# Expert weights in rows of 1024 columns: one change to a two-layer transformer trunk on one core

## The reference

```python
def swiglu(x, w_gate, w_up, w_down):
    return (jax.nn.silu(x @ w_gate) * (x @ w_up)) @ w_down

def moe_swiglu(x, router, w_gate, w_up, w_down):
    logits = (x @ router).astype(jnp.float32)
    top_vals, top_idx = lax.top_k(logits, TOP_K)          # 2 of 8 experts for each frame
    gates = jax.nn.softmax(top_vals, axis=-1)
    combine = jnp.sum(jax.nn.one_hot(top_idx, N_EXPERTS) * gates[..., None], axis=-2)
    y = jnp.zeros_like(x)
    for e in range(N_EXPERTS):
        y = y + combine[..., e:e + 1] * swiglu(x, w_gate[e], w_up[e], w_down[e])
    return y
```

## Time and profile before

| | |
|---|---|
| median of 3 runs | 1616.21 us (1614.83 to 1619.98) |
| the profiled execution | 1619.26 us, its span 1617.5 us |
| TensorE, matmul / weight load | 95% / 80% of the span busy |
| VectorE, ScalarE, GpSimd | 78%, 64%, 8% busy |
| DMA | 484.32 MB, 299 GB/s over the span |
| the expert part, from about 662 us on | 388 GB/s in most slices |

### The profile page before, as it was taken

How to read it: one execution, slowest core, us unless ns; L and a number is a source line. 1 busy time by engine, 2 the same in 40 slices (tenths; PEclk the granted TensorE clock), 3 DMA queues, 4 the chain that set the end, 5 groups by cost and what they waited for, 6 DMA issues and landing times.

```text
span 1617.5 us, 22158 instructions
## 1 busy us (share of the span) xinstructions
PE 1541.0 (95%) x7950; PEld 1286.4 (80%) x7950; DVE 1260.5 (78%) x1224; ACT 1041.4 (64%) x972; POOL 126.6 (8%) x148
## 2 busy tenths in 40 slices
PE   9999999999999898999999999998999998999886
PEld 9888988888896797788888888776887776887664
DVE  5687475555647565789889889899898889898988
ACT  5564444443436443678778777887777887778774
POOL 3103010000104201000000000000000000000220
PEclk9999999999999999899999999999999999999988
DMA  9437856465465462799999999999999999999994
GB/s 356 167 131 239 308 176 221 137 219 187 168 210 181 141 211 66 251 385 335 390 388 387 388 379 369 388 387 387 388 387 388 388 387 387 388 387 389 381 381 173
DMA packets 239042, 484.32 MB, mean 299 GB/s; under 512 B 8352, under 2 KB 11456, under 8 KB 238944
## 3 DMA queue, kind: packets, MB, share of 16 engines
q1 hardware_dynamic: 229744, 454.06, 78.1%
q0 software_dynamic: 7440, 25.83, 4.9%
q10 hardware_dynamic: 1760, 3.15, 0.5%
HBM read 477.21 MB, written 14.18 MB: 304 GB/s over the span
## 4 chain that ended last, share of the span: by engine, by line
PE 61%; DVE 14%; DMA 12%; issue 8%; ACT 3%; POOL 1%; SPq 0%; DVEq 0%; ACTq 0%; POOLq 0%
PE bank L427 16%; PE bank L429 16%; PE bank L428 16%; DVE w_lo L2150 4%; DMA raw<-in_moe_w_up_dram 3%; DMA raw<-in_moe_w_down_dram 3%; DMA raw<-in_moe_w_gate_dram 2%; PE bank L417 2%; PE bank L420 2%; PE bank L419 2%; ACT w_hi L1183 2%; DMA c_add<-gate_rows 2%; DVE w_lo L1593 2%; DVE w_lo_more L2150 1%; PE bank L906 1%
## 5 line engine op out<-in xcount | busy, mean ns | idle before, releaser
L1183 ACT ACTIVATE w_hi<-raw 128x2048 fp32r<-128x2048 f32 (+1 forms) x322 | 608.2, 1894 | 236.5 <-PE bank L429 161.6
L2150 DVE TENSOR_TENSOR w_lo<-raw,w_hi 128x2048 fp32r<-128x2048 f32 x221 | 502.3, 2288 | 69.2 <-ACT w_hi L1183 64.8
L1593 DVE TENSOR_TENSOR w_lo<-raw,w_hi 128x2048 fp32r<-128x2048 f32 (+1 forms) x96 | 211.1, 2203 | 144.4 <-ACT w_hi L1183 144.1
L427 PE MATMUL bank<-w_hi,xe_hi 128*128 128x512 f32 x460 | 182.8, 397 | 0.2
L429 PE MATMUL bank<-w_hi,xe_lo 128*128 128x512 f32 x460 | 179.6, 390 | 0.0
L428 PE MATMUL bank<-w_lo,xe_hi 128*128 128x512 f32 x460 | 179.2, 390 | 0.0
L2150 DVE TENSOR_TENSOR w_lo_more<-raw,w_hi_more 128x2048 fp32r<-128x2048 f32 x63 | 144.1, 2288 | 15.0 <-ACT w_hi_more L1183 9.4
L427 PE MATMUL bank<-w_hi,xT_hi 128*128 128x512 f32 (+1 forms) x384 | 146.9, 383 | 0.1
L429 PE MATMUL bank<-w_hi,xT_lo 128*128 128x512 f32 (+1 forms) x384 | 144.5, 376 | 0.0
L428 PE MATMUL bank<-w_lo,xT_hi 128*128 128x512 f32 (+1 forms) x384 | 144.4, 376 | 0.0
L1183 ACT ACTIVATE w_hi_more<-raw 128x2048 fp32r<-128x2048 f32 x64 | 122.8, 1918 | 23.2 <-PE bank L429 7.9
(11 more groups left out here) (356 smaller groups left out, 3023.1 us busy)
## 6 DMA issues: line engine op xcount, KB each, us to landing
raw<-in_moe_w_gate_dram SPq DMA_DIRECT2D x96, 1024.0 KB, 11.3
raw<-in_moe_w_up_dram SPq DMA_DIRECT2D x96, 1024.0 KB, 11.0
raw<-in_moe_w_down_dram SPq DMA_DIRECT2D x96, 1024.0 KB, 11.4
raw<-in_mem_wkv_dram SPq DMA_DIRECT2D x16, 1024.0 KB, 7.4
raw_more<-in_moe_w_up_dram SPq DMA_DIRECT2D x16, 1024.0 KB, 13.5
raw_more<-in_moe_w_gate_dram SPq DMA_DIRECT2D x16, 1024.0 KB, 10.7
raw_more<-in_moe_w_down_dram SPq DMA_DIRECT2D x16, 1024.0 KB, 12.0
raw<-in_c_w_in_dram SPq DMA_DIRECT2D x12, 1024.0 KB, 5.1
```

The costliest lines, as they stand in the source:

```text
L427: nc.tensor.matmul(d, xh, hi[:, k, :], start=(first and k == 0), stop=False)
L1183: return nc.scalar.activation(dst, src, ACT.Copy)
L1593: tt(w_lo[s][:, 0:n], raw[c % NRAW][:, 0:n], w_hi[s][:, 0:n].bitcast(F32), ALU.subtract).then_inc(lo_made, 1)
L2150: tt(w_lo[s][:, :], raw_exp[r][:, :], w_hi[s][:, :].bitcast(F32), ALU.subtract).then_inc(lo_made, 1)
```

## The change

The expert weights of a chunk become two row tiles by 1024 columns instead of four row tiles by 512. The chunk is as large as before and there are as many; its contiguous rows in HBM are 4 KB. With 1024 columns a chunk feeds two banks: gate blocks 2i and 2i + 1 are filled together by four chunks, then both up blocks by four; in down the left and the right half of the output, banks 4 and 5, fill together over 14 chunks. Seven blocks are three pairs and an odd one, which stays at 512 columns, and so do the down chunks of the last job, whose left half is wanted early.

```diff
+        def gate_up(c):
+            if c < 8 * DBL:                      # DBL = EJ // 2 = 3 pairs, RK = CK // 2 = 2 row tiles
+                up, q = divmod(c % 8, 4)
+                return up, (2 * (c // 8), 2 * (c // 8) + 1), RK * q, RK, q == 0, q == 3
+            up, q = divmod(c - 8 * DBL, 2)
+            return up, (EJ - 1,), CK * q, CK, q == 0, q == 1
...
+                if idx is not None and len(outs) == 2:
+                    both = [w[s][:, :].rearrange("p (k c) -> p k c", k=n) for w in (w_hi, w_lo)]
+                    for k in range(n):
+                        for i, (_, dst) in enumerate(outs):
+                            wh, wl = (w[:, k, i * cols:(i + 1) * cols] for w in both)
...
+                            nc.tensor.matmul(dst[:, :], xh, wh, start=begin, stop=False)
+                            nc.tensor.matmul(dst[:, :], xh, wl, start=False, stop=False)
+                            m = nc.tensor.matmul(dst[:, :], xl, wh, start=False, stop=end)
...
-                    src = w[0][bass.ds(e, 1), k0 * P:(k0 + CK) * P, col:col + W].rearrange(
+                        w, k0, n, col = moe_w_down, RK * (c - 4 * EJ), RK, 0
+                    src = w[0][bass.ds(e, 1), k0 * P:(k0 + n) * P, col:col + CHUNK // n].rearrange(
                         "e (k p) c -> p (e k) c", p=P)
```

More of the change, by code:

```diff
@@ L859, in expert @@
                     idx = N0 + c + EC * job
-                    if c < 2:
-                        pe.wait_ge(emptied[c], start[c] + JOB_CLAIMS[c] * job)
+                    if c == 0:
+                        for b in range(2):
+                            pe.wait_ge(emptied[b], start[b] + JOB_CLAIMS[b] * job)
                     if c == C_INDEX:
@@ L874, in expert @@
                     if c < 4 * EJ:
[L875 to L880, removed]
+                        up, js, k0, _, first_of, last_of = gate_up(c)
+                        outs = [(0, bank[2 * up + j % 2]) for j in js]
+                        if first_of:
+                            for j in js:
+                                claim(pe, f"{z}eu{j}" if up else f"{z}eg{j}", 2 * up + j % 2, job,
+                                      signal=False)
+                        chunk_product(c, outs, xe_hi, xe_lo, k0, first_of, last_of, W, idx=idx,
+                                      slot=E_SLOT[c], done=chunk_used,
                                       packed=(lambda k: xe_two[:, k, :]) if narrow else None)
-                    else:
+                    elif last:
                         i, q = divmod(c - 4 * EJ, EK // CK)
@@ L891, in expert @@
                                       packed=(lambda k: eT_two[:, k, :]) if narrow else None)
-                    if c % 4 == 1 and 1 <= c // 4 <= EJ:
-                        j = c // 4 - 1
+                    else:
+                        q = c - 4 * EJ
+                        if q == 0:
+                            for i in range(2):
+                                claim(pe, f"{z}ed{i}", 4 + i, job, signal=False)
+                        if q % 2 == 0:
+                            wait_emptied(pe, f"{z}et{q // 2}", job)
+                        chunk_product(c, [(0, bank[4]), (0, bank[5])], eT_hi, eT_lo, RK * q, q == 0,
+                                      c == EC - 1, W, idx=idx, slot=E_SLOT[c], done=chunk_used,
+                                      packed=(lambda k: eT_two[:, k, :]) if narrow else None)
+                    if c in C_FOLD:
+                        j = C_FOLD[c]
                         b = 6 + j % 2
@@ L1507, in expert @@
                         nc.scalar.nop().then_inc(emptied[fillings[f"{z}eu{j}"][0]], 1)
-                    if (c == 4 * EJ + EK // CK - 1 or c == EC - 1) and (last or not narrow):
-                        i = (c - 4 * EJ) // (EK // CK)
+                    for i in range(2):
+                        if c != (EC - 1 if i or not last else C_HALF) or (narrow and not last):
+                            continue
                         act.wait_ge(chunk_used, idx + 1)
@@ L2134, in expert @@
                         nc.vector.nop().then_inc(emptied[fillings[f"{z}eu{j}"][0]], 1)
-                    if narrow and not last and (c == 4 * EJ + EK // CK - 1 or c == EC - 1):
-                        i = (c - 4 * EJ) // (EK // CK)
+                    for i in range(2):
+                        if c != EC - 1 or last or not narrow:
+                            continue
                         dve.wait_ge(chunk_used, idx + 1)
```

85 lines of the change are left out of this document (52 added, 33 removed).

## The result

The change made the kernel slower by 0.6%: 1626.98 us (six runs, 1624.55 to 1627.76) against 1618.41 us for the kernel before in the same comparison, a ratio of 1.0058 [1.0047, 1.0069]. Forecast were 1606 and a range of 1595 to 1617. The profiled execution is 1627.3 us long, its span 1625.6.

A forecast was written before the change was run, and what follows sets the result against it. The DMA was taken to pace the pairs n1+w1 and n2+w2, TensorE the wide jobs ahead, VectorE z. Terms -4.4, -6.5, -2, -0.5 and +3.6 gave -9.8, say -10: median 1616.2 becomes 1606, range 1595 to 1617.

The forecast's parts named there:

- The stream: Weight loads in 4 KB rows: 410 GB/s instead of 388; n1 -4.4, n2 -6.5, w1 and w2 together -2 us.
- z: Last job, bound by VectorE with down chunks as before: 0 to -1 us, taken as -0.5.
- Transposed blocks are wanted one for two chunks of down, not one for each: never late: Down chunks: paired chunks want transposed blocks less often, so no wait for them; 0 us.
- The paired evacuations: 0: Bank readouts of paired blocks, followed through steps 19 to 29: 0.7 us or more in hand at each chunk, cost 0.
- VectorE reads both halves at step 41 ... 0: Narrow job's y readout: the same work, 1.4 us passing into the next wide job's start; -1.4 and +1.4, net 0.
- 1.2 us each: ScalarE's second y piece at step 41 of wide jobs delays the starts of n1, n2 and z: 3.6 us in all.
- Slower: Rival, chance 0.07: pairs cost TensorE its lead in wide jobs' three-slot steps, +21 us less the 10: 1627.

The follow-up runs named there:

- rows only: Kernel before, its program kept, most chunks loaded as two row tiles by 1024 columns (weights in wrong places, timing only): 1605.62 us, ratio 0.9922.
- down only: Changed kernel with gate and up back at 512 columns in the old order, only down weights at 1024, both y halves at step 41: 1619.84 us.
- experiment 6: Changed kernel with the odd block folded into bank 3 instead of bank 6, no instruction moved: 1621.21 us, ratio 1.0024 to the kernel before.
- 2 to 7: Changed order with 512-column loads; changed kernel with later odd fold, y behind split, down at 512, bank 3, or bank 3 and y late: 1616.75 to 1631.88 us.
- 1 and 8 to 10: Long rows alone; down alone at 1024; that with y late; the latter with ScalarE's y piece cut to 8 columns: 1605.62, 1619.84, 1612.93, 1613.49 us.
- experiment 7: Kernel of experiment 6, with VectorE reading a narrow job's first y half in step 6 of the following wide job: 1616.75 us, ratio 0.9995.
- experiment 5: Changed kernel with down weights of every job at 512 columns again and y's halves at steps 34 and 41: 1625.03 us, ratio 1.0039.

## Why the prediction was wrong, step by step

**What paces a narrow job.** Its length is VectorE's busy time and VectorE's idle time. In n1 it is busy for 98.7 us with the rows alone and for some 97.6 in the changed kernel, since one half of y has moved out. The idle time of n1 and n2, added up from the gaps between VectorE's instructions in each trace and cut at its splits, shows where each kernel loses:

| us | length | idle | up to the split of chunk 4 | 4 to 19 | 19 to 30 | 30 to 34 | rest |
|---|---|---|---|---|---|---|---|
| n1, rows only | 103.7 | 5.0 | 2.6 | 0.2 | 2.0 | 0.0 | 0.3 |
| n1, down only | 104.2 | 7.1 | 3.9 | 0.9 | 2.0 | 0.0 | 0.3 |
| n1, down at 512 | 109.5 | 10.4 | 2.6 | 0.6 | 4.5 | 2.5 | 0.3 |
| n1, bank 3 | 106.8 | 9.2 | 3.9 | 0.6 | 4.7 | 0.0 | 0.0 |
| n1, changed | 110.9 | 13.3 | 3.9 | 0.6 | 4.7 | 4.1 | 0.0 |
| n2, rows only | 107.4 | 8.7 | 6.2 | 0.2 | 2.0 | 0.0 | 0.3 |
| n2, down only | 108.6 | 11.2 | 7.6 | 0.2 | 2.5 | 0.5 | 0.3 |
| n2, down at 512 | 114.8 | 15.7 | 6.2 | 0.6 | 4.6 | 4.0 | 0.3 |
| n2, bank 3 | 111.1 | 13.4 | 8.2 | 0.6 | 4.7 | 0.0 | 0.0 |
| n2, changed | 114.3 | 16.4 | 8.1 | 1.3 | 4.5 | 2.4 | 0.0 |

**The stream: right.** 403 to 412 GB/s where nothing holds it, n1 103.7 us with the rows alone (103.6 forecast), n2 107.4 (106.5), w1 and w2 119.6 (119). That the median of the rows alone, 1605.6, meets the forecast of 1606 is luck: this kernel moves no y piece, so its forecast is the sum without the 3.6 us for them, 13.4 us less than before. Measured are 12.9 less in the same comparison, so the step itself was well sized. The one term off there is z, 1.8 us longer instead of 0.5 shorter.

**"Transposed blocks are wanted one for two chunks of down, not one for each: never late": this step failed.** It asks when a block is wanted, and not when the bank it comes in is free. What it says holds: before, TensorE waits 3.7 us in n1 for the last block, at chunk 34,

```profile
PE bank L408 <- DVE eT_two L2166: 3.7, 1, 3.7
```

and in the changed kernel that chunk takes 1.8 us instead of 7.5. But pairs bring the folds of blocks 4 and 6 from eight chunks apart to four, and the stop stands at chunk 30 instead. n1, n2 and z lose 4.1, 3.2 and 2.7 us by it (experiment 6; 6 us in all by the medians), where the forecast had 0. In the table it is the column from 30 to 34.

**"The paired evacuations: 0": right for wide jobs, not counted for narrow ones.** I followed steps 19 to 29 in wide jobs only; wide 1 and 2 stayed at 119.0 us. In narrow jobs VectorE is idle for 2.7 us more from its split of chunk 19 to that of chunk 30 (4.7 against 2.0), in n1 as in n2. The seven kernels that pair gate and up (changed, 2 to 7) have 4.5 to 5.1 us there in n1 and n2; the four that load long rows but keep the old order of gate and up (1 and 8 to 10) have 2.0 to 4.1, six of eight values at 2.0 to 2.5. So the pairs cost it. ScalarE and then VectorE there, in the kernel of experiment 7:

```profile
1080.91 0.60 ACT L1232 ACTIVATE e_h<-bank 128x512 f32<-128x512 f32 x1 [0.75 <-PE bank L425]
1081.68 1.92 ACT L1232 ACTIVATE w_hi<-raw 128x2048 fp32r<-128x2048 f32 x1 [0.17 <-ACT e_h L1232]
1083.50 0.58 ACT L1232 ACTIVATE e_h<-bank 128x512 f32<-128x512 f32 x1
```
```profile
1083.63 2.29 DVE L2205 TENSOR_TENSOR w_lo<-raw,w_hi 128x2048 fp32r<-128x2048 f32 x1 [0.98 <-ACT w_hi L1232]
```

Both up blocks of a pair are copied out in successive steps, each ahead of a split, and VectorE waits for the splits. Which of these copies matters was not taken apart.

**"VectorE reads both halves at step 41 ... 0": failed.** It was balanced as -1.4 and +1.4. The piece that left a narrow job took about 1.1 us of VectorE's busy time out of it, but the one that came to the start of w1 and w2 cost 1.6 us each (experiments 5 and 7), 4.5 us in all by the median of experiment 7.

**"1.2 us each" for ScalarE's second piece: right in kind, somewhat small.** ScalarE and VectorE at the start of n1 in the changed kernel:

```profile
1019.10 0.60 ACT L1232 ACTIVATE y<-bank 128x512 f32<-128x512 f32 x1 [0.88 <-PE bank L430]
...
1020.38 0.60 ACT L1232 ACTIVATE y<-bank 128x512 f32<-128x512 f32 x1 [0.69 <-ACT y L1232]
...
1021.58 1.92 ACT L1232 ACTIVATE w_hi_more<-raw 128x2048 fp32r<-128x2048 f32 x1 [0.60 <-ACT y L1232]
```
```profile
1023.53 2.29 DVE L2200 TENSOR_TENSOR w_lo_more<-raw,w_hi_more 128x2048 fp32r<-128x2048 f32 x1 [2.99 <-ACT w_hi_more L1232]
```

VectorE's idle time there was 1.62 us and is 2.99: 1.4 more; in n2 and z it is 1.7 more. Experiment 5, where the piece stands at step 34, has the idle time of rows only up to the split of chunk 4 (2.6 and 6.2 in the table), against 3.9 and 8.1: the piece costs 1.3 us in n1, 1.9 in n2 and, from the same sum in z (2.6 and 4.3), 1.7, together 4.9 where 3.6 were forecast. TensorE waits twice and falls to half clock within the next chunk:

```profile
1025.88 0.50 PE L424 MATMUL bank<-w_hi_more,xe_two 128*128 128x512 f32 x1 [1.46 <-DVE w_lo_more L2200]
...
1029.58 0.60 PE L857 MATMUL bank<-token_no,pick 128*128 128x1 f32 x4 [1.58 <-DVE pick L2015]
...
1031.24 0.63 PE L425 MATMUL bank<-w_lo,xe_two 128*128 128x512 f32 x1
1031.67 0.63 PE L424 MATMUL bank<-w_hi,xe_two 128*128 128x512 f32 x1
```

Chunks 3 and 4 of n1 took 9.2 us instead of 6.4. But this half clock cost n1 nothing. The kernel of experiment 6 has the same program there, its clock stayed at 1.00 and the two chunks took 7.7 us, and yet its VectorE starts the split of chunk 20 at the same place, 46.5 us behind the end of wide 2. Up to there VectorE has hardly any idle time in either kernel (0.6 us from chunk 4 to 19), and TensorE makes its delay good behind it.

**The rivals.** "Slower" had the right time, 1627, by the wrong mechanism: it put the loss into three-slot steps of the wide jobs, which lost nothing. The loss is in the narrow jobs and in the starts behind them. Its chance of 0.07 was too low because each zero was given for itself, and none was tried in the jobs where VectorE has no idle time to spare.

By the jobs, the changed kernel stands 20.2 us above the rows alone in n1 to z: 10.2 go with the bank (experiment 6), 1.0 with VectorE's y (experiment 7), and 9.0 stay. By the medians it is 21.4 us: 5.8, 4.5 and 11.1. Of what stays, the table shows two causes in n1 and n2, ScalarE's second piece and the pairs of gate and up; what stays in z is not taken apart.

## What to carry to other kernels

When a block of work is merged into a larger one, list for every buffer who frees it and how many steps lie between its two uses before and after; a consumer's deadline says nothing of that. Do the count in the stage where the pacing engine has least idle time, and price a wait of another engine by what reaches the pacing one: a wait of TensorE of 1.5 us with half clock behind it cost that engine nothing beyond the late split that had caused both, and one of 2.8 us cost it 4.1, most of that through the lower clock. If the gain is in the transfers, first change the operands whose new order disturbs the other engines least: here the down weights alone, with VectorE's y late, gave the better kernel.

## What the runs showed of the hardware

- With transfers of the same 1 MB the stream ran at 388 GB/s in rows of 2 KB and at 408 to 412 in rows of 4 KB where nothing held it up, with 44208 and some 25600 packets for two jobs. The mean share of the sixteen engines in n1 was 1.05 before and 1.03 with the rows alone, at 387 and 404 GB/s.
- One idle time of 2.8 us of TensorE was followed by 6.9 us at half clock (from 1098.44 to 1105.3), in which TensorE did what took 3.6 us in experiment 6.
- An ACTIVATE of 8 columns took 0.18 us and one of 512 took 0.60, but the step from one piece to the next took 0.86 and 1.28: some 0.7 us of it does not go with the size: the wait behind its own write, in which the store is issued.
